# The order of VectorE's and ScalarE's work around a seven-product up projection

## The reference

```python
def modulate(x, w, shift, scale):
    return rmsnorm(x, w) * (1 + scale[:, None, :]) + shift[:, None, :]

def sqrelu_mlp(h, w1, w2):          # w1: 1024 x 4096, w2: 4096 x 1024
    a = jax.nn.relu(h @ w1)
    return (a * a) @ w2
...
        h = modulate(x, norm2_w[i], sh2, sc2)
        x = x + g2[:, None, :] * sqrelu_mlp(h, mlp_w1[i], mlp_w2[i])
```

## Time and profile before

| | us |
|---|---|
| median of 3 runs | 1368.43 |
| lowest and highest run | 1366.80, 1368.76 |
| the profiled execution, its own time | 1368.77 |
| its span in the profile | 1367.0 |
| TensorE busy | 1337.8 |
| VectorE busy | 831.9 |
| ScalarE busy | 556.7 |

### The profile page before, as it was taken

The page is one execution under the profiler, slowest core; times in us unless marked ns, Lnnn a source line. Parts: engine busy times, 40 slices in busy tenths (PEclk is TensorE's granted clock), DMA queues, the critical chain, the costliest instruction groups (busy, mean ns, idle before and its releaser), DMA issues.

```text
span 1367.0 us, 22617 instructions
## 1 busy us (share of the span) xinstructions
PE 1337.8 (98%) x8566; PEld 1186.3 (87%) x8566; DVE 831.9 (61%) x1482; ACT 556.7 (41%) x866; POOL 172.2 (13%) x220
## 2 busy tenths in 40 slices
PE   7999999999999999999999999999997999999997
PEld 6889898989988888888899898987797988899887
DVE  6785666656775556663366667666668832478333
ACT  5624241414533113432236454535446732267321
POOL 7351515241100000000001101010020000000000
PEclk9999999999999999999999999999998999999999
DMA  9363434313465556552214232322222333233311
GB/s 368 143 217 123 139 116 145 120 53 94 144 219 175 184 184 234 195 186 92 93 63 156 63 93 68 103 63 72 69 63 78 107 112 105 65 105 122 110 62 62
DMA packets 47506, 169.58 MB, mean 124 GB/s; under 512 B 5168, under 2 KB 7344, under 8 KB 46912
## 3 DMA queue, kind: packets, MB, share of 16 engines
q1 hardware_dynamic: 46816, 164.21, 36.3%
q10 hardware_dynamic: 608, 4.23, 0.9%
HBM read 166.29 MB, written 2.13 MB: 123 GB/s over the span
## 4 chain that ended last, share of the span: by engine, by line
PE 87%; DVE 7%; ACT 3%; issue 3%; POOL 0%; DMA 0%; ACTq 0%; DVEq 0%; POOLq 0%
PE bank L1038 20%; PE bank L1040 20%; PE bank L1039 20%; PE bank L1156 4%; PE bank L1157 4%; PE bank L1158 4%; PE bank L1235 2%; PE bank L1495 2%; PE bank L1465 2%; DVE wlo L1657 1%; PE bank L1479 1%; PE bank L1254 1%; PE bank L1224 1%; ACT whi L480 1%; ACT whi L476 1%
## 5 line engine op out<-in xcount | busy, mean ns | idle before, releaser
L463 ACT ACTIVATE whi<-raw 128x1024 fp32r<-128x1024 f32 x176 | 185.6, 1055 | 248.7 <-PE bank L1040 230.8
L1649 DVE TENSOR_TENSOR wlo<-raw,whi 128x1024 fp32r<-128x1024 f32 x177 | 219.2, 1252 | 11.1 <-ACT whi L463 11.1
L962 POOL TENSOR_TENSOR rst<-ssq,mhalf 128x8 f32<-128x8 f32 (+2 forms) x29 | 42.8, 1485 | 1066.9 <-DVE ssq L1593 892.1
L1038 PE MATMUL bank<-a1hi,whi 128*128 128x512 f32 (+1 forms) x288 | 105.7, 367 | 0.3
L1038 PE MATMUL bank<-h1hi,whi 128*128 128x512 f32 (+1 forms) x288 | 105.5, 366 | 0.0
L1038 PE MATMUL bank<-a0hi,whi 128*128 128x512 f32 (+1 forms) x288 | 105.4, 366 | 0.0
L1040 PE MATMUL bank<-a1hi,wlo 128*128 128x512 f32 (+1 forms) x288 | 105.3, 366 | 0.0
L1039 PE MATMUL bank<-a1lo,whi 128*128 128x512 f32 (+1 forms) x288 | 105.3, 365 | 0.0
L1039 PE MATMUL bank<-h1lo,whi 128*128 128x512 f32 (+1 forms) x288 | 105.3, 365 | 0.0
L1039 PE MATMUL bank<-a0lo,whi 128*128 128x512 f32 (+1 forms) x288 | 105.2, 365 | 0.0
L1040 PE MATMUL bank<-a0hi,wlo 128*128 128x512 f32 (+1 forms) x288 | 105.2, 365 | 0.0
(11 more groups left out here) (313 smaller groups left out, 3559.0 us busy)
## 6 DMA issues: line engine op xcount, KB each, us to landing
raw<-stream SPq DMA_DIRECT2D x208, 512.0 KB, 4.2
mring<-mod_rows SPq DMA_DIRECT2D x80, 512.0 KB, 3.7
modf<-mod_rows SPq DMA_DIRECT2D x16, 512.0 KB, 15.2
fb<-negf ACTq DMA_DIRECT2D x4, 1024.0 KB, 6.3
x<-x_t SPq DMA_DIRECT2D x4, 512.0 KB, 5.8
out_t<-x SPq DMA_DIRECT2D x8, 256.0 KB, 2.2
wf<-w_forget SPq DMA_DIRECT2D x1, 512.0 KB, 4.6
par<-params SPq DMA_DIRECT2D x1, 86.0 KB, 2.0
```

What stands on the lines that cost most here:

```text
L463: S.activation(whi[:, slot_of(quad, j, more), :], raw[:, j, :], ACT.Copy).then_inc(w_hi, 1)
L962: G.tensor_tensor(rst[:, at:at + n], ssq[:, at:at + n], mhalf[:, 0:n], ALU.pow).then_inc(done, 1)
L1038: PE.matmul(out, wh, hh[0], start=first, stop=False, skip_group_check=shared)
L1649: V.tensor_tensor(wlo[:, w, :], raw[:, j, :], whi[:, w, :].bitcast(F32), ALU.subtract).then_inc(w_lo, 1)
```

## The change

It reorders the second layer's up projection and moves some of its tiles; TensorE's instructions and their order stay as they are.

- VectorE's queue: the first two weight sums of group 37 are computed in the norm, between the last low of group 36's weights and the second half's normed tokens. Then the four input sums, their lows and the lows of group 37's weights are interleaved: input sum 0, low 0, input sum 1, its lows, and so on. Input sum 3 and its low move into group 37 (`opening`), behind its Z seed. The lows of the plain outputs move behind weight sum 3 of group 38.
- ScalarE's queue: the highs of group 37's weights and the input highs come before or between the evictions of the plain group. The plain group's Squares and Copies, and input highs 2 and 3, move into group 37, between its highs. In every group Square and Copy of an output follow its eviction at once.
- The outputs are evicted into `av`, which lies where `a1lo` lies; Square works there, and the low is written over the value that it is computed from. Evictions no longer wait for lows.
- In a later group output 2's low follows weight sum 4, output 3's low comes behind the Z seed and low 6, and outputs 0's and 1's lows come behind the next group's sum 3.
- Weight sum 3 is written over B12 in its `raw` slot, and that slot is loaded again when the low of the sum is done. B22 is the third block of a group in the stream and B21 the fourth.
- `vsb` takes the place of a scratch tile.

The diff, cut to its core (the memory of `av`, and lines that repeat for another engine, are left out):

```diff
-B11, B12, B21, B22 = range(4)
+B11, B12, B22, B21 = range(4)
...
+        def outputs(t, tl, pos):
+
+            n_tile, th = ((0, 0), (1, 1), (1, 0), (0, 1))[pos]
+            return t[:, 4 * tl + n_tile:4 * tl + n_tile + 3:2, part(th)]
+
...
-                used = [(t_rdy, 4 * i + 1), (t_rdy, 4 * i + 3), (t_rdy, 4 * i + 4), (w_lo, item(q - 1, 5) + 1)]
-                for j in range(4):
-                    sp.wait_ge(*used[j])
+                summed = {B11: 1, B12: 3, B22: 3, B21: 4}
+                lowered = {B11: 0, B12: 4, B22: 5, B21: 3}
+                for j in (B11, B12, B21, B22):
+                    sp.wait_ge(t_rdy, 4 * i + summed[j])
+                    sp.wait_ge(w_lo, item(q - 1, lowered[j]) + 1)
                     weight(q, j)
...
-                    at, t = {1: (1, 0), 2: (2, 1), 4: (3, 0), 6: (4, 1)}[s]
+                    at, t = {1: (1, wsum[0][:, :]), 2: (2, wsum[1][:, :]), 4: (3, raw[:, B12, :]), 6: (4, wsum[1][:, :])}[s]
                     act.wait_ge(t_rdy, 4 * i + at)
-                    S.activation(whi[:, n % 4, :], wsum[t][:, :], ACT.Copy).then_inc(w_hi, 1)
+                    S.activation(whi[:, n % 4, :], t, ACT.Copy).then_inc(w_hi, 1)
...
             def mlp_products(layer, a, h, shift):
                 base = layer * LAYER_QUADS + Q_MLP
-                out_of = [scr[0], scr[1], sqb, acc]
-
-                def evict(quad, n0, pos):
+
+                def evict(quad, tl, n0, pos):
 
                     i = UP_QUADS.index(quad)
                     x_, y_, v_ = bank_set(i)
-                    act.wait_ge(ff_lo, n0 + pos - (1 if not seven(quad - 1) and pos < 2 else 3))
+                    out = outputs(av, tl, pos)
                     if pos == 1:
                         act.wait_ge(w_out_sb, i + 1)
                     else:
                         act.wait_ge(pe_blk, item(quad, {0: 3, 2: 5, 3: 6}[pos]) + 1)
-                    S.activation(out_of[pos][:, :], (ps[x_], scr[1], ps[v_], ps[y_])[pos][:, :], ACT.Relu,
+                    S.activation(out, out if pos == 1 else pairs(ps[(x_, None, v_, y_)[pos]][:, :]), ACT.Relu,
                                  scale=-1.0 if pos == 3 else 1.0).then_inc(ff_r, 1)
...
+                    S.activation(value, value, ACT.Square).then_inc(ff_sq, 1)
+                    act.wait_ge(ff_sq, n + 1)
+                    S.activation(high, value, ACT.Copy).then_inc(ff_hi, 1)
+
+                def squared(tl, n0, pos):
+                    split_ff(n0 + pos, outputs(av, tl, pos), outputs(a[0], tl, pos))
+
+                def input_high(m):
+
+                    act.wait_ge(ah_32, m + 1)
+                    S.activation(ah[0][:, m, :, :], a32[:, m, :, :], ACT.Copy).then_inc(ah_hi, 1)
+
+                def plain_evict(quad, j):
+
+                    act.wait_ge(pe_blk, item(quad, j) + 1)
+                    S.activation(tile(av, j), ps[j][:, :], ACT.Relu).then_inc(ff_r, 1)
+
+                def plain_squared(j):
+                    split_ff(32 * layer + j, tile(av, j), tile(a[0], j))
...
+                    opening = tl > 0 and not late
                     act.wait_ge(pe_blk, item(quad, 0) + 1)
+                    if opening:
+                        act.wait_ge(ff_r, 32 * layer + 4)
                     S.activation(ps[y_][:, :], ps[x_][:, :], ACT.Copy, scale=-1.0).then_inc(y_seed, 1)
+                    if opening:
+                        input_high(2)
                     hi_behind(quad, 0)
                     if late:
-                        upper_ff(n0 - 4, tl - 1, 2)
-                        evict(quad - 1, n0 - 4, 3)
+                        evict(quad - 1, tl - 1, n0 - 4, 3)
+                        squared(tl - 1, n0 - 4, 3)
+                    if opening:
+                        plain_squared(0)
                     act.wait_ge(pe_blk, item(quad, 1) + 1)
                     if i:
                         act.wait_ge(w_out_sb, i)
                     S.activation(vsb[:, :], ps[v_][:, :], ACT.Copy).then_inc(v_out, 1)
                     hi_behind(quad, 1)
-                    if late:
-                        squared(n0 - 1, acc)
-                        upper_ff(n0 - 4, tl - 1, 3)
+                    if opening:
+                        plain_squared(1)
+                        input_high(3)
                     hi_behind(quad, 2)
+                    if opening:
+                        plain_squared(2)
+                        plain_squared(3)
                     hi_behind(quad, 3)
-                    evict(quad, n0, 0)
-                    squared(n0, scr[0])
+                    evict(quad, tl, n0, 0)
+                    squared(tl, n0, 0)
                     hi_behind(quad, 4)
-                    upper_ff(n0, tl, 0)
+                    evict(quad, tl, n0, 1)
+                    squared(tl, n0, 1)
                     hi_behind(quad, 5)
-                    evict(quad, n0, 1)
-                    squared(n0 + 1, scr[1])
-                    evict(quad, n0, 2)
+                    evict(quad, tl, n0, 2)
+                    squared(tl, n0, 2)
                     hi_behind(quad, 6)
-                    upper_ff(n0, tl, 1)
-                    squared(n0 + 2, sqb)
                     if not seven(quad + 1):
-                        upper_ff(n0, tl, 2)
-                        evict(quad, n0, 3)
-                        squared(n0 + 3, acc)
-                        upper_ff(n0, tl, 3)
-
-                for s in range(4):
-                    act.wait_ge(ah_32, s + 1)
-                    S.activation(ah[0][:, s, :, :], a32[:, s, :, :], ACT.Copy).then_inc(ah_hi, 1)
-                plain(base)
+                        evict(quad, tl, n0, 3)
+                        squared(tl, n0, 3)
+
+                hi_behind(base, 0)
+                input_high(0)
+                plain_evict(base, 0)
+                hi_behind(base, 1)
+                input_high(1)
+                plain_evict(base, 1)
+                hi_behind(base, 2)
+                plain_evict(base, 2)
+                hi_behind(base, 3)
+                plain_evict(base, 3)
                 for half in range(2):
                     for tl in range(1 - half, 4):
+                        if half == 0 and tl == 2:
+                            act.wait_ge(ah_lo, 4)
                         products(base + 8 * half + tl, half, tl)
...
-                    ins = V.tensor_tensor(wsum[0][:, :], raw[:, B12, :], raw[:, B22, :], ALU.add)
+                    ins = V.tensor_tensor(raw[:, B12, :], raw[:, B12, :], raw[:, B22, :], ALU.add)
...
+                    if kept(n):
+                        weight_sum(q0 + 3, 1)
+                        weight_sum(q0 + 3, 2)
...
+            def input_sum(n, h, shift, m):
...
+                def input_low(m):
+
+                    dve.wait_ge(ah_hi, m + 1)
+                    V.tensor_tensor(ah[1][:, m, :, :], a32[:, m, :, :], ah[0][:, m, :, :].bitcast(F32),
+                                    ALU.subtract).then_inc(ah_lo, 1)
+
+                def lower_ff(n, low, value, high):
+
+                    dve.wait_ge(ff_hi, n + 1)
+                    V.tensor_tensor(low, value, high.bitcast(F32), ALU.subtract).then_inc(ff_lo, 1)
+
+                def plain_low(j):
+                    lower_ff(32 * layer + j, tile(a[1], j), tile(av, j), tile(a[0], j))
+
+                def low_out(tl, n0, pos):
+                    lower_ff(n0 + pos, outputs(a[1], tl, pos), outputs(av, tl, pos), outputs(a[0], tl, pos))
...
+                    opening = tl > 0 and not late
                     lower_behind(quad, 0)
-                    weight_sum(quad, 4)
-                    lower_behind(quad, 1)
-                    if late:
-                        lower_ff(n0 - 4, tl - 1, 3)
-                    dve.wait_ge(pe_blk, item(quad, 2) + 1)
-                    dve.wait_ge(v_out, i + 1)
-                    V.tensor_tensor(ps[v_][:, :], ps[y_][:, :], vsb[:, :], ALU.add).then_inc(z_seed, 1)
-                    lower_behind(quad, 2)
-                    lower_behind(quad, 3)
-                    if on:
+                    if opening:
+                        dve.wait_ge(pe_blk, item(quad, 2) + 1)
+                        dve.wait_ge(v_out, i + 1)
+                        V.tensor_tensor(ps[v_][:, :], ps[y_][:, :], vsb[:, :], ALU.add).then_inc(z_seed, 1)
+                        input_sum(2 * layer + 1, h, own_shift, 3)
+                        lower_behind(quad, 1)
+                        weight_sum(quad, 4)
+                        input_low(3)
+                        lower_behind(quad, 2)
+                    else:
+                        weight_sum(quad, 4)
+                        if late:
+                            low_out(tl - 1, n0 - 4, 2)
+                        lower_behind(quad, 1)
+                        dve.wait_ge(pe_blk, item(quad, 2) + 1)
+                        dve.wait_ge(v_out, i + 1)
+                        V.tensor_tensor(ps[v_][:, :], ps[y_][:, :], vsb[:, :], ALU.add).then_inc(z_seed, 1)
```

(45 more changed lines are left out.)

98 lines of the change are left out of this document (32 added, 66 removed).

## The result

The changed kernel takes 1358.88 us (median of 4 runs, 1358.57 to 1359.79), the kernel before 1368.6 in 4 runs beside it: a ratio of 0.9932, with an interval of 0.9915 to 0.9949. In a later set of runs it took 1359.4 against 1367.7, 0.9941 (0.9928 to 0.9955). The forecast was 1360.7.

The account below looks back on a forecast made before the run. TensorE, busy 98% of the span, bounds the kernel; gains come from its waits and slow clock. 6.5 + 1.2 + 0.55 - 0.5 = 7.75 us off 1368.77 gives 1361.0, median 0.34 lower: 1360.7 us; range 1356.3 to 1365.5.

Parts of the forecast that it names:

- What bounds the kernel: Whole kernel: TensorE is busy 98% of the span, so time can only come from its waits or slow stretches.
- Two sums into the norm's wait: Norm before group 37: two weight sums, 2.4 us, fit VectorE's 3.28 us idle and cost nothing; 0.3 kept for the root.
- B22 as the third load: Norm's second sum: B22 is there by 1011.6; past a landing of 1012.8 each microsecond costs one.
- B12 summed in place: Weight loads in each group: slot free some 6 us in, load has until 13.7 us; worth nothing.
- The opening of group 37: Group 37's start: waits of 4.93 and 2.26 us go, a new 0.5 us wait comes; group ends 10.4 us earlier.
- Group 38 gives back 4 us: Group 38: third to fifth products wait 2.2, 1.05 and 1.6 us; of 10.4 us, 6.5 remain gained.
- Groups 44 to 47: Second half's groups: the Z seed, late behind the last output's low, comes over 1 us early; 1.2 us gained.
- The last lows: End of each half: last lows finish before the down group's second block, 0.28 us each, 0.55 us for two.
- Clock: Behind group 38's waits: a clock fall costs 1.5 us; 0.5 us deducted, between 0 and 3.1.
- Rival (a): Group 38 doesn't wait: all 4.9 us of its waits would be gone, giving 1355.8 us; chance 0.10.

Follow-up runs that it names:

- old opening: Changed kernel with VectorE's and ScalarE's opening queues in the order of the kernel before; two sums stay in the norm, evictions in `av`: 1360.99 us, 0.9944.
- with them moved: Changed kernel with Squares, Copies and output lows of groups 37 to 39 two outputs later, plus group 38's output sum one place earlier: 1354.49 us, 0.9903.
- the run with the splits: Changed kernel with Squares and Copies of groups 37 to 39 two outputs behind their evictions, group 38's Y seed and low 3 earlier: 1354.83 us, 0.9903.

## Why the prediction was right

The direction, the places and the mechanism came out as written; two terms were smaller mistakes. The forecast of 1360.7 us is 1.8 above the median measured. Of that, 0.54 is the scatter ahead of the changed stretch, 0.5 the clock and 0.18 the last lows (both below); the remaining 0.6 is that the profiled execution lies 0.91 above its kernel's median, where that of before lay 0.34. The first and the last are luck.

- *What bounds the kernel*: one reading was off. The waits on line 2050 are not among the three longest kinds; between 4.9 and their 2.0 stand 3.2 on line 1066, 2.3 on line 1082, the Y seed's 2.3 and 2.0 on line 1075. The argument doesn't hang on it.
- *Two sums into the norm's wait*: right. They ran at 1010.10 and 1011.43 and cost the norm nothing (4.56 against 4.57 us without them); taken out, 2.29 us come back. The root went as the row said: by its record it ended at 1010.74, inside the first sum, 1.84 us after the read of the squares' sum and no later than without the sums. The second sum started 1.33 us after the first, 0.2 more than usual, of which the prediction had 0.13, for it waits until the first has ended; 0.8 of idle time were left behind it. The rule of the Trainium skill's page "SBUF — State Buffer" (Who interferes with whom), by which the root could have waited for both sums, gave 0.3; the runs give nothing.
- *B22 as the third load*: right, and its price too: one microsecond for each past the point (1.88 late, 1.89 lost).
- *B12 summed in place*: right; from 1010 to 1275 neither TensorE, VectorE nor ScalarE waited for a load. What it is worth by itself was not tried.
- *The opening of group 37*: right to a tenth or two. Less the 0.54 that this execution was early, the first high was predicted for 1021.96 (measured 1021.99), low 0 for 1023.06 (1023.08), the Y seed for 1030.86 (1030.82), the Z seed for 1036.76 (1036.76). The wait before the sixth product was 0.29 for 0.5.
- *Group 38 gives back 4 us*: right. Waits of 2.10, 0.89 and 1.46 against 2.2, 1.05 and 1.6. The gain of the first half is 6.43, predicted 6.5. The old opening shows what "given back" means: with 7 us of stall and slow clock returned, the half is only 1.81 longer. So of the 6.43 the opening's order alone is worth 1.81 and the place of the two sums alone 2.29, each with the rest of the change in place.
- *Groups 44 to 47*: 1.20 us, as predicted; the reason given was half of it. The output's low ahead of the seed alone costs 0.6 of 1.6 us of margin and no time. The prediction left out weight sum 3 behind a waiting low, which takes the whole margin; only then does the low cost its 0.6 as well.
- *The last lows*: 0.40 + 0.33 = 0.73, predicted 0.55. The prediction priced the one late triple (0.97 us to its start instead of 0.68); in the kernel before, the next one took 0.77 as well. That the lateness hangs on ScalarE's order is shown for the second down group: with that order back, in both runs the two triples take 0.96 or 0.97 and 0.77 again, and the rest of the span 99.30 and 99.25 against 98.95. For the first down group it was not tried.
- *Clock*: the term that was mis-sized. I took 0.5 off for a fall in group 38. In the changed kernel the clock stayed at 1.00, and where it did fall there it cost nothing (below). With 0 in its place the sum is 8.25; with the 0.54 of scatter and the 0.2 of the lows that is the measured 8.9 within 0.1.
- *Rival (a)*, a group 38 without waits: my argument against it was that ScalarE's work in group 37 exceeds TensorE's time whatever the order. That holds for group 37 alone. The splits can wait for two groups, and with them moved the waits went: 1354.49 us, near the 1355.8 of that rival, which stood for the kernel as it was.

## What to carry to other kernels

When an engine's queue is over-full for one group of a pipeline, reordering within the group only moves the stall to the next; look for work with the latest due time (here Squares, Copies and output lows) and let it trail by a group or two. An instruction that another engine needs early doesn't belong behind one that waits for that same engine: follow the queue from the waiting instruction to the next thing that the other side lacks. Margins add up: two moves that each fit, or nearly fit, into the slack of a seed can cost time together. Time a stage from an event just ahead of it to one just behind, and a fraction of a microsecond can be read from a single execution, where whole runs scatter by one to three; but look at TensorE's pace first, for 84.03 and 82.97 are the same kernel.

## What was not expected of the hardware

The clock's fall behind a wait of 2.1 us came in three of the nine executions that have that wait, and cost nothing there. With VectorE's, with ScalarE's and with the lows' old order in groups 44 to 47 (a later stretch) it fell in group 38: four triples of 0.640 us. The window and the third and fifth product of the last of these runs:

```profile
1056.00:1072.00 16.00, 14.96 (x113) 14.75 (x113) 14.56 (x17) 10.71 (x16) 0.00 (x0) 0.89 0.40 132
```

```profile
1055.13 0.39 PE L1060 MATMUL bank<-ahhi,whi 128*128 128x256 f32 x1 [2.10 <-ACT bank L763]
...
1063.66 0.38 PE L1060 MATMUL bank<-ahhi,whi 128*128 128x256 f32 x1 [1.04 <-DVE bank L2098]
```

From the third to the fifth product it takes 8.53 us with the fall, 8.51 in the changed kernel without one (1056.05 to 1064.56): the fourth product's wait vanished and the fifth's shrank from 1.46 to 1.04, for what both wait for comes from VectorE's queue, which was just as late with either clock: the Z seed starts 54.93 us after the read of the squares' sum with the fall and 54.92 without. In the run with the old opening, where no wait came behind the slow triples, they cost their 2.0 us.

TensorE's pace at a granted clock of 1.00 is 0.3533 or 0.340 us per triple and changes only where a product starts, mostly behind a wait; the changed kernel had 79 triples at the one in one execution and at the other in another, worth 1.05 us. Ahead of a wait that another engine ends, the faster pace is worth next to nothing, as the 46 triples in the run with the splits show. What chooses is open.
